# Modulation moved ahead of the transposes in four of the norms of a three-layer fp32 kernel

## The reference

```python
def _rms(x, g):
    y = x * lax.rsqrt(jnp.mean(x * x, axis=-1, keepdims=True) + EPS)
    return y * g

h  = _rms(x, g_attn_pre[l]) * (1.0 + sc_a) + sh_a
...
x  = x + gt_a * _rms(y, g_attn_post[l])
hf = _rms(x, g_ffn_pre[l]) * (1.0 + sc_f) + sh_f
x  = x + gt_f * _rms(_swiglu(hf, w_gate, w_up, w_down), g_ffn_post[l])
```

## Time and profile before

| | |
|---|---|
| median of 3 runs | 2424.91 us (2424.83 to 2428.48) |
| the profiled execution's own time | 2427.63 us |
| its span in the profile | 2425.9 us |
| mean granted TensorE clock | 0.953 |
| PE busy | 2186.5 us (90%) |
| DVE busy | 1729.5 us (71%) |
| ACT busy | 1141.7 us (47%) |
| POOL busy | 63.7 us (3%) |
| moved by DMA | 438.73 MB, mean 181 GB/s |

### The profile page before, as it was taken

How to read it: one execution, slowest core, us unless ns; L and a number is a source line. 1 busy time by engine, 2 the same in 40 slices (tenths; PEclk the granted TensorE clock), 3 DMA queues, 4 the chain that set the end, 5 groups by cost and what they waited for, 6 DMA issues and landing times.

```text
span 2425.9 us, 37881 instructions
## 1 busy us (share of the span) xinstructions
PE 2186.5 (90%) x14634; PEld 1963.7 (81%) x14634; DVE 1729.5 (71%) x3415; ACT 1141.7 (47%) x1935; POOL 63.7 (3%) x79
## 2 busy tenths in 40 slices
PE   3998799999999999989987979799989988797998
PEld 3987799999987778879865656799979978567997
DVE  5667679889977877788866566577776665665554
ACT  2543354545554444444444445544454445354444
POOL 1000000000000000000011000000000000000000
PEclk9999999999999999999988889899999998898999
DMA  7648646664468887777741110477767753103664
GB/s 286 204 139 280 203 142 197 217 195 150 144 199 269 263 261 246 272 236 238 249 107 40 53 52 18 148 251 251 246 209 255 255 162 119 53 1 122 186 187 131
DMA packets 139218, 438.73 MB, mean 181 GB/s; under 512 B 15712, under 2 KB 38496, under 8 KB 138528
## 3 DMA queue, kind: packets, MB, share of 16 engines
q1 hardware_dynamic: 109440, 396.93, 51.2%
q10 hardware_dynamic: 25776, 23.97, 2.9%
q0 software_dynamic: 3824, 15.40, 1.8%
HBM read 422.58 MB, written 13.66 MB: 180 GB/s over the span
## 4 chain that ended last, share of the span: by engine, by line
PE 49%; DVE 14%; issue 11%; DMA 9%; ACT 4%; POOL 1%; ACTq 0%; DVEq 0%; POOLq 0%; SPq 0%
PE bk L1718 46%; DVE SPL L1129 4%; DMA RAW<-in_peer 4%; DMA TMP<-kept 3%; PE bk L1724 3%; ACT SPL L787 2%; DVE RAW L1163 1%; DVE R L1129 1%; DVE TMP L1129 1%; DVE ST L1144 1%; ACT R L789 1%; DMA HID<-kept 1%; DVE R L1138 1%; DVE EXT L1163 1%; POOL ST L664 1%
## 5 line engine op out<-in xcount | busy, mean ns | idle before, releaser
L1129 DVE TENSOR_TENSOR SPL<-RAW,SPL 128x1024 fp32r<-128x1024 f32 (+1 forms) x614 | 744.3, 1218 | 365.7 <-ACT SPL L787 364.4
L787 ACT ACTIVATE SPL<-RAW 128x1024 fp32r<-128x1024 f32 (+1 forms) x614 | 644.8, 1054 | 623.2 <-PE bk L1718 275.7
L1718 PE MATMUL bk<-HH,SPL 128*128 128x256 f32 x3840 | 747.9, 288 | 27.5 <-DVE HL L1129 13.7
L1718 PEld LDWEIGHTS bk<-HH,SPL 128*128 128x128 f32 x3840 | 621.0, 194 | 36.4 <-DVE HL L1129 14.3
L1718 PE MATMUL bk<-SPL,WHL 128*128 128x512 f32 x2328 | 555.2, 392 | 13.6 <-DVE WHL L1129 9.4
L1718 PE MATMUL bk<-HL,SPL 128*128 128x256 f32 x1920 | 547.3, 285 | 0.0
L1718 PEld LDWEIGHTS bk<-SPL,WHL 128*128 128x128 f32 x2328 | 429.5, 188 | 107.2 <-issue 19.4
L1718 PEld LDWEIGHTS bk<-HL,SPL 128*128 128x128 f32 x1920 | 372.7, 194 | 2.2
L1718 PE MATMUL bk<-SPL,HH 128*128 128x256 f32 (+1 forms) x1664 | 317.7, 293 | 31.1 <-DVE SPL L1129 19.3
L1718 PEld LDWEIGHTS bk<-SPL,HH 128*128 128x128 f32 x1664 | 271.0, 200 | 40.5 <-issue 26.3
L787 ACT ACTIVATE R<-bk 128x512 f32<-128x512 f32 (+4 forms) x344 | 168.1, 500 | 200.8 <-PE bk L1718 175.9
(11 more groups left out here) (130 smaller groups left out, 1953.3 us busy)
## 6 DMA issues: line engine op xcount, KB each, us to landing
RAW<-in_peer SPq DMA_DIRECT2D x256, 512.0 KB, 4.7
RAW<-in_ada SPq DMA_DIRECT2D x144, 512.0 KB, 4.7
RAW<-in_ffn SPq DMA_DIRECT2D x132, 512.0 KB, 4.2
RAW<-in_win SPq DMA_DIRECT2D x96, 512.0 KB, 4.7
RAW<-in_ffd SPq DMA_DIRECT2D x66, 512.0 KB, 4.3
RAW<-in_wout SPq DMA_DIRECT2D x32, 512.0 KB, 4.8
kept<-TMP ACTq DMA_DIRECT2D x88, 128.0 KB, 3.0
TMP<-kept ACTq DMA_DIRECT2D x66, 128.0 KB, 5.5
```

The costliest lines, as they stand in the source:

```text
L787: ins = e.activation(out, in_, func, bias=bias, scale=scale)
L1129: e.tensor_tensor(out, a, b, op).then_inc(*dve.up(*points))
L1718: ins = e.matmul(out, lhsT, rhs, start=start, stop=stop, skip_group_check=True)
```

## The change

For four of the seven norms of the layers, (0,0,"f"), (0,1,"f"), (1,0,"a") and (1,0,"f"), A and B are spread over all partitions as rows by way of DRAM (`keep_row`, `row_of`), and applied to the tokens before the transposes. `norm_k` multiplies x by the row A, half 0 ahead of the wait for the sums and half 1 behind the instruction that POOL waits for; `norm_b` then writes (x A) r + B. The transposed banks need no arithmetic any more, and are taken by `turn_hi` and `turn_lo`, as in the merge. ACT's squares in `an_b` write to another scratch tile, since xn is now written earlier. `PLAN` is unchanged.

```diff
--- before.py
+++ after.py
@@ -417,6 +417,9 @@
                                   for s in ((1, 0) if both else (0,))]
 
         VECS = {"peer": 0, (0, 0, "a"): 1, (0, 0, "f"): 2, (0, 1, "a"): 3, (0, 1, "f"): 4, (1, 0, "a"): 5, (1, 0, "f"): 6}
+        ROWNORM = {(0, 0, "f"): 17088, (0, 1, "f"): 13188, (1, 0, "a"): 20416, (1, 0, "f"): 17088}
+        for t in ROWNORM:
+            VECS[t + ("A",)], VECS[t + ("B",)] = len(VECS), len(VECS) + 1
         first_ctx = PLAN.index(("norm_b", (0, 1, "a")))
         in_ext = {CHUNKS[s][0] for s in PLAN[:first_ctx] if s[0] == "ada"}
         mods = {}
@@ -607,6 +610,9 @@
             if (l, s) != (1, 1):
                 NORM[(l, s, "f")] = dict(x3=LX[s], xn=q["oY"], ht=q["junk"], A=m["FA"], B=m["FB"], s=s)
 
+        for t, a in ROWNORM.items():
+            NORM[t]["Ar"], NORM[t]["Br"] = R[:, a:a + 1024], R[:, a + 1024:a + 2048]
+
         def ss_of(t):
 
             s = NORM[t]["s"]
@@ -734,10 +740,23 @@
                     for s in ((0, 1) if l == 0 else (0,)):
                         keep_row((l, s, "a"), mods[(l, s)]["ga"])
                         keep_row((l, s, "f"), mods[(l, s)]["gf"])
+                        keep_row((l, s, "f", "A"), mods[(l, s)]["FA"])
+                        keep_row((l, s, "f", "B"), mods[(l, s)]["FB"])
+                elif l == 1:
+                    pool.wait_ge(T.at("mods", 1, "a"))
+                    keep_row((1, 0, "a", "A"), mods[(1, 0)]["A"])
+                    keep_row((1, 0, "a", "B"), mods[(1, 0)]["B"])
+                    norm_rows((1, 0, "a"))
+
+            def norm_rows(t):
+                for n in ("A", "B"):
+                    row_of(t + (n,), NORM[t][n + "r"])
 
             def gB(l, s, k):
                 pool.wait_ge(T.at("full", ("av", l, s, 5)) if k == "a" else T.at("scaled", ("op", l, s, 3)))
                 row_of((l, s, k), QS[(l, s)]["gB"])
+                if k == "a":
+                    norm_rows((l, s, "f"))
 
             def c_in():
                 pool.wait_ge(T.at("mul", ("peer", 99)), T.at("saved"))
@@ -831,6 +850,9 @@
 
             def nT(t, i, k):
                 n = NORM[t]
+                if t in ROWNORM:
+                    turn_hi(("nT", t, i, k), H[n["s"]], i, k)
+                    return
                 ht3, Hs = v2(n["ht"], 8), H[n["s"]]
                 c = slice(i * P, (i + 1) * P)
                 if k == 0:
@@ -1084,7 +1106,7 @@
             def an_b(l, s, k):
                 for i in range(2):
                     act.wait_ge(T.at("x3" if i else "x3a", l, s, k))
-                    A(v2(QS[(l, s)]["oY"], 2)[:, i, :], LX[s][:, i, :], ACT.Square, ("ssn", l, s, k),
+                    A(v2(QS[(l, s)]["junk"], 2)[:, i, :], LX[s][:, i, :], ACT.Square, ("ssn", l, s, k),
                       accum=stat(6 + i, 1, s))
 
             def fs(l, s, j):
@@ -1175,11 +1197,11 @@
                 stt(r, y, 1.5, r, ALU.add, ALU.mult)
                 dve.wait_ge(dve.own)
 
-            def turn_lo(key, Hs, i, k):
+            def turn_lo(key, Hs, i, k, *points):
                 c = slice(i * P, (i + 1) * P)
                 dve.wait_ge(T.at("turned", *key))
                 tt(Hs[1][:, 4 * k:4 * k + 4, c], v2(ps(*key), 4), Hs[0][:, 4 * k:4 * k + 4, c].bitcast(F32),
-                   ALU.subtract, ("out", key))
+                   ALU.subtract, ("out", key), *points)
 
             def rope(x4, cs, sn, n, half, tmp, *points):
                 c = v2(cs, 2).unsqueeze(2).to_broadcast([P, 2, n, half])
@@ -1256,8 +1278,16 @@
 
             def norm_k(t):
                 l, s, k = t
-                dve.wait_ge(T.at("ssn", l, s, "a") if k == "f" else T.at("ssn", l - 1, s, "f"))
-                mean_eps(ss_of(t)[0], D, "norm", t)
+                before = ("ssn", l, s, "a") if k == "f" else ("ssn", l - 1, s, "f")
+                n = NORM[t]
+                for i in range(2):
+                    if t in ROWNORM:
+                        if i == 0:
+                            dve.wait_ge(T.at("row", t + ("A",)), dve.own)
+                        tt(v2(n["xn"], 2)[:, i, :], n["x3"][:, i, :], n["Ar"], ALU.mult)
+                    if i == 0:
+                        dve.wait_ge(T.at(*before))
+                        mean_eps(ss_of(t)[0], D, "norm", t)
 
             def norm_b(t):
                 n, (a, r, y) = NORM[t], ss_of(t)
@@ -1266,10 +1296,17 @@
                     if t == "fin":
                         dve.wait_ge(T.at("fn"))
                         stt(n["x3"][:, i, :], n["x3"][:, i, :], r[:, i:i + 1], fn, ALU.mult, ALU.mult, ("fin",))
+                    elif t in ROWNORM:
+                        dve.wait_ge(T.at("row", t + ("B",)))
+                        x = v2(n["xn"], 2)[:, i, :]
+                        stt(x, x, r[:, i:i + 1], n["Br"], ALU.mult, ALU.add, ("xn", t, i))
                     else:
                         ts(v2(n["xn"], 2)[:, i, :], n["x3"][:, i, :], r[:, i:i + 1], None, ALU.mult, None, ("xn", t, i))
 
             def nT(t, i, k):
+                if t in ROWNORM:
+                    turn_lo(("nT", t, i, k), H[NORM[t]["s"]], i, k, ("hT", t, i))
+                    return
                 if k == 0:
                     return
                 n, key = NORM[t], ("nT", t, i, 1)
@@ -2121,7 +2158,7 @@
         xs = nc.dram_tensor("xs", (P, 2048), F32, kind="Internal").ap()
         out = nc.dram_tensor("out_0", (1, 256, D), F32, kind="ExternalOutput").ap()
         kept = nc.dram_tensor("kept", (NA, P, 256), F32, kind="Internal").ap()
-        vec = nc.dram_tensor("vec", (7, D), F32, kind="Internal").ap()
+        vec = nc.dram_tensor("vec", (15, D), F32, kind="Internal").ap()
         program(nc, dram, out, xs, kept, vec, points)
         return nc
```

## The result

The changed kernel takes 2436.93 us (median of 14 runs, 2428.04 to 2440.30), the kernel before 2426.65 us (14 runs on the same chip, 2420.32 to 2432.30): ratio 1.0039, 95% interval 1.0029 to 1.0049. By the ratio it is 9.5 us slower (by the medians 10.3) where 10.5 us less were forecast, and it lies outside the range.

What follows compares the result with a forecast made beforehand. PE bounds the feed-forwards, so its pauses at the four norms were to shrink: 4.7 + 4.4 + 0.9 + 2.0 - 0.5 - 1.0 = 10.5 us off the 2424.9 median, giving 2414.4 us. Range 2409 to 2420.5.

Steps and rivals of the forecast that it cites:

- the rows by way of DRAM: Eight added 512 KB reads and eight small writes: no row waited for, cost 0, at the most 2 us.
- signs that it gave for being wrong: In the profile after: a 1.4 us power, DVE waiting for a row, a pause inside a feed-forward, or a longer feed-forward.
- The rival that ended slower: The added reads' 4.2 MB, 17.7 us of transfers, are not hidden; kernel 7 us slower, 2432; chance 0.04.
- (0,1,"f") and (1,0,"f"): Last norm and its like: mean to first product shortens by 2.35 us each, 4.7 for both.
- (0,0,"f"): Norm woven into the context's feed-forward: PE's pause falls from 9.13 to 4.7 us, 4.4 gained.
- TensorE's clock at the cold norms: At the last norm and (0,1,"f"): products start from 1.2 GHz as now, no gain taken.
- The clock gives more: Rival: low-clock stretches behind the last norm and (0,1,"f") shrink, up to 4 us more, 2410.4; chance 0.13.
- (1,0,"a"): Norm in layer 1: 3.5 us gained, 2.6 lost, net 0.9; clock returns 2.0, longer pause at 1993 costs 0.5.
- POOL's power: Beside half 1's multiplication at three norms: delay between 0 and 0.7 us, 0.35 taken each, 1.0 in all.
- The sum: All terms: 4.7 + 4.4 + 0.9 + 2.0 - 0.5 - 1.0 = 10.5 us gained.

Runs made afterwards that it cites:

- w8_before: Kernel before plus the eight added row writes, never read, norms as before; 2438.36 against 2423.80 us, ratio 1.0058.
- r8_after: Changed kernel without its eight added writes, the eight reads fetching gate rows instead; 2414.26 us, ratio 0.9953.
- pk15_after: pk8_after with the seven rows of the kernel before also written in 128 pieces each; 2433.59 us, ratio 1.0043.
- mv3_after: mv4_after with (1,0,"a") also back in its old form, so no write at 1790; 2416.22 us, ratio 0.9976.
- no10a_after: Changed kernel with (1,0,"a") back in its old form, its two writes and reads gone; 2422.89 against 2423.47 us before, ratio 1.0008.
- pk8_after: Changed kernel with the eight added rows written in 128 pieces each, DVE reading them with a step of 8; 2427.05 us, ratio 1.0010.
- mv4_after: Changed kernel with six writes moved behind POOL's last power of each layer's attention, the two at 1790 staying; 2419.98 us, ratio 0.9989.
- mv3_late: mv3_after with the two row reads for (0,0,"f") issued later, with the gate row of (0,1,"f"); 2414.84 against 2427.43 us before, ratio 0.9944.
- mv3_lock: mv3_after with half 1's multiplication by A moved from `norm_k` to `norm_b`, behind half 0's addition; 2415.62 us, ratio 0.9974.

## Why the prediction was wrong

**The step that failed: the rows by way of DRAM.** The prediction took 0, at the most 2, for eight reads and "eight small writes". It asked whether a new row would be late for its reader ("So the rows wait for nothing", which holds for the eight new rows), and not what the writes do to others in the same DMA engines. Counted by bytes, 32 KB were nothing. The runs show for the writes 13.3 us from 1241 on (w8_before), and 19.8 between the changed kernel and r8_after (8.1 and -11.7), in place of 0; for the reads 1.3 to 2.4 us, in place of 0 and at the edge of its 2. It had named their way, the context's gate row that is now fourth of six, but counted on the ring to cover it. Three of the signs that it gave for being wrong are there: a power over 1.4 us (1.60), a DVE instruction that waits for a row (6.58, for the gate row) and a pause in the middle of a feed-forward (6.10). The rival that ended slower had the wrong carrier: it let the 4.2 MB of reads fail to hide, and r8_after has all of them and gains 11.7.

A sign stood in the trace of before: behind its four writes the DMA engines moved 39 GB/s for 16 us at a share of 0.58. It cost nothing there, and a cost that is covered is not read off the path. The Trainium skill (DMA: Bandwidth & Descriptors, section "Rules for kernel authors") says that a strided last dimension becomes one descriptor per element, and that it should be rearranged so that it is contiguous. The runs agree that the layout matters: eight writes in a row land after 22.0 us element by element and after 2.2 to 2.8 in 128 pieces each (pk15_after), two at 1790 after 9.8 (the first, w8_before) and 1.7.

**The norms.** (0,1,"f") and (1,0,"f"): 2.35 less 0.35 each were forecast, that is 2.0; measured 1.8 (10.69 to 8.89) at the last, less the 0.38 by which its mean came later, and from 1547 to the power at 1683, around the first, 1.9 in the changed kernel and 0.8 to 3.4 in the experiments that have it in this form. (0,0,"f"): 4.4 - 0.35 forecast; from 1683 to 1866, where no write stands at 1790, 5.4 to 6.9 (mv3_after and no10a_after at the ends). The pause gives 4.9 (9.13 to 4.23) of it. The rest is the clock, for which nothing was taken here. Behind the pause, before and with the change:

```profile
1778.50:1784.70 6.20, 6.17 (x29) 6.18 (x30) 4.53 (x10) 3.83 (x6) 0.00 (x0) 0.50 0.01 3
```

```profile
1785.80:1786.40 0.60, 0.55 (x4) 0.55 (x5) 0.33 (x2) 0.00 (x0) 0.60 (x2) 1.00 0.07 27
1786.40:1790.00 3.60, 3.60 (x20) 3.60 (x19) 3.24 (x7) 2.03 (x3) 0.09 (x1) 0.53 0.36 146
```

6.2 us at half clock became 3.6, about 1.3 us more; in mv3_after, the kernel with the least gain here, 5.3 us were left.

**TensorE's clock at the cold norms.** The prediction took no gain there and gave the rival "The clock gives more" 0.13. It came in part. At the last norm the stretch at half clock behind the first product fell from 5.5 us to 2.9 to 3.8 in eight of the ten kernels with the new form, in one (pk8_after) to 4.2, and in mv4_after to nothing. At (0,1,"f"), where it was 3.2 us before, it stayed at 2.9 to 4.4 in eight, and in mv3_after and mv3_late the first product already ran at full clock: these are the two that gain 2.0 and 2.1 from 1547 to 1723 where the others gain 0.3 to 0.6 (pk8_after and pk15_after apart, which pay for the step of 8). The prediction held against this rival that transposes stand ahead and not products. In mv3_late the clock rose within the 16 transposes, from 0.50 to 0.78 and then to 1.00:

```profile
1560.00:1560.60 0.60, 0.54 (x4) 0.26 (x2) 0.44 (x2) 0.47 (x2) 0.00 (x0) 0.78 1.05 430
1561.95:1563.00 1.05, 1.05 (x9) 1.05 (x10) 0.85 (x1) 0.16 (x1) 0.00 (x0) 1.00 0.00 0
```

What decides between the two cases isn't shown: the pause between the transposes and the first product is 1.41 us in both.

**(1,0,"a")** was mis-sized. The sum had 0.9 + 2.0 - 0.5 = 2.4 for it. The pause (5.47 to 1.95) and the full clock behind it came as forecast. The keys' transposes wait 3.3 us longer where 2.6 were put, since the power of 1.60 us leaves DVE another wait of 0.59 behind half 1. And the low clock from there on, taken at 0.5, costs more in two of the three kernels: over the 5.7 us behind 1994 the granted clock is 0.82 before and 0.55 in r8_after, 1.5 us. From 1866 to the power at 2057, r8_after gains 1.1, mv4_after 0.9 and the changed kernel 1.9. The table's stretch goes on to 2094 and takes in the 1.5 us at 2057 that have nothing to do with the norm. Kernels with this norm unchanged gain 0.8 us up to 2057 as well (no10a_after, mv3_after, mv3_lock): the keys' transposes ran at full clock there, 1.05 us for eight where the kernel before took 1.91, behind the same pause of 1.38. So the norm is worth 0.1 to 0.3 us by pairs of kernels (r8_after and no10a_after, mv4_after and mv3_after), and 0.9 to 1.9 against the kernel before; more can't be said with one profile of each.

**POOL's power.** 0.35 each was taken, between 0 and 0.7. It took 1.60 us in all four norms for 0.69 to 0.80, and 2.39 beside the multiplication of 2.0 us in pk8_after: each time it ends some 0.55 us after the multiplication. That is a full wait, as the rule has it that the prediction cites from the Trainium skill (SBUF — State Buffer, section "SBUF: two separate sides"). The single row of 0.80 that was weighed against it bounded nothing, since the DVE instruction beside it was short:

```profile
1722.64 0.42 DVE L1129 TENSOR_TENSOR WHL<-R,WHL 128x256 fp32r<-128x256 f32 x1
```

The wait delays by 0.8 to 0.9; taking it away gave 0.16, since the multiplication must stand somewhere.

**The sum.** The terms of the norms made 10.5, and without the writes 11.7 were measured by profile and 11.4 by ratio. That the two are so close is in part luck: 1.5 us of the 11.7 are the clock at 2057, some 2 to 3 the clock behind (0,0,"f") and the last norm, and against them stand 1.6 lost to the reads and 1.3 to 1.5 less at (1,0,"a"). With 19.8 for the writes by profile the changed kernel is 8.1 slower from 1241 on, 9.5 by ratio.

**What stays open**: beside the clock, why r8_after and mv3_after, with sums of -11.7 and -12.2, stand at ratios of 0.9953 and 0.9976. The stretch ahead of 1241 wanders by up to 10 us with equal code, and the intervals are 6 to 7 us wide; nothing here tells chance from a cause.

## What to carry to other kernels

Count a small DMA by its pieces and look at what shares the DMA engines with it, not at its bytes or at whether its own reader waits: eight writes of 4 KB, element by element, cost more than eight reads of 512 KB. Few GB/s while loads are issued and not landed are the mark of it, with a DMA share of 0.80 in one place and 0.27 in another; if it costs nothing today, ask how much more fits under the same cover. The same writes were free where nothing was being loaded, which was the cheaper remedy than another layout, because the layout moved the step to DVE.
